# The products with the 16 meta keys in softmax attention: one stacked product of 96 rows for both heads

## The chip, the cores and the metric

One of the eight cores of a Trainium2 chip runs the whole program. The metric is the device time of one execution in microseconds, the median of several runs. The kernel before takes 2984.65 us (2983.28 to 2986.08 in 3 runs).

## The reference, cut to what matters

The program computes two blocks of a language model on 512 tokens, with 16 meta tokens in front, in float32. The first block has two layers (DEPTH = 2). In each, four branches of width 256 are computed from one projection: A, a windowed attention with a sink and a bias; B, an attention with rotary positions; C, a differential attention (two softmaxes, the second subtracted with the factor lam); D, a gated linear attention. In A, B and C every query sees the 16 meta keys beside its own keys. For A this reads

```python
s_b = jnp.einsum('bnqhgd,bnkhd->bhgnqk', qb, kb).astype(jnp.float32) * scale + head_bias(rel_b)
s_m = jnp.einsum('bnqhgd,bmhd->bhgnqm', qb, km).astype(jnp.float32) * scale + head_bias(rel_m)
p = jax.nn.softmax(jnp.concatenate([s_b, s_m, s_sink], axis=-1), axis=-1).astype(v.dtype)
p_b = p[..., :3 * BLOCK]
p_m = p[..., 3 * BLOCK:3 * BLOCK + N_META]
o = jnp.einsum('bhgnqk,bnkhd->bnqhgd', p_b, vb) + jnp.einsum('bhgnqm,bmhd->bnqhgd', p_m, vm)
```

and B and C are softmax attention over all 528 keys. Each has four query heads and two key and value heads of 64. The second block has a windowed attention of its own (kind W) without meta keys.

## The kernel before

The tokens are cut into tiles (TILES): four of 128 and, last, one of the 16 meta tokens; layer 1 leaves the meta tile out as a query tile. The list `att` has one entry for each step of the softmax attention: a query tile and a pair of heads, one for each of the two key heads (j = 0, 1). A layer runs all steps of C, then of A, then of B: 30 steps in layer 0 and 24 in layer 1. Kind C has four cells a step (two softmaxes for each head), A and B have two. A cell is one row of scores for a query, its meta part first (16 columns) and then the other keys.

The engines walk the same list, each in its own order, tied by semaphores. Every engine executes its instructions in the order written.

TensorE (`attention`, L1776 on) makes at step n the scores of n (`scores`, L1633; for B and C the scores against the meta keys by a product of its own at L1644, for both heads at once), then the values products of n - 2 (`values`, L1687), then turns the probabilities of n - 1 (`turn_probs`, L1657): a transpose of the 16 meta columns of each head (L1681) into bank 5 of the accumulators, and one transpose for each 128 other keys (L1684) into bank 4. Then it fills up with products of other branches (`fill_piece`, L1728, 24 products of fp32r type at L1742 to L1750), and at last come the transposes of the second head. Around B, `turn_heads` (L1714) turns the rotated queries and keys of one tile per step through bank 7.

In `values`, 128 keys at a time of both heads are multiplied with the values (128 rows, 64 columns of weights, so that the two heads lie beside one another in the array), and then, for the last group, the 16 meta keys of each head (16 rows): `v` is the values' part in the work buffer, and `x` is PT for the 128-row groups and PTM for the meta group (L1709, L1710). All of it is plain fp32, each product in two passes, hence two records in the trace. At odd steps the reciprocals of the sums are spread first (L1696). Elsewhere in the kernel exact products are made of three fp32r ones: the operand is split into a high part (rounded to fp32r) and a low part (the difference).

ScalarE (`attention`, L2587 on) makes the exps (L2503), copies the turned probabilities into PT (L2517, first and second head) and right after the first head's copy the turned meta probabilities of both heads into PTM, a part of the buffer `cross` (L2520), then copies the finished group (L2526), the fills and the turned heads (`copy_heads`, L2529), and rounds weights (L2243).

VectorE (`attention`, L3377 on) makes at step n the ratios of the sums (L3321, L3324) and, in C, the difference of the two softmaxes (L3335) of step n - 1, the meta scores (L3301, L3306) and their minimum (`meta_scores`, L3293, one reduce at L3309 for all cells), one minimum for each cell with the scores written beside it (`minima`, L3285), the scaling of a finished group (L3359), then rotary work (L3252 to L3267), gates and the low halves of weights (L2935). GpSimd has the rotary products (L1213 to L1220).

## Time and profile before

| | |
|---|---|
| median of 3 runs | 2984.65 us |
| lowest, highest | 2983.28, 2986.08 us |
| span of the profiled execution | 2989.1 us |
| softmax attention of layer 0 | about 99 to 292 us |
| softmax attention of layer 1 | about 1153 to 1322 us |

How to read it: the page gives busy time of every engine, the chain of work that ended last, and groups of instructions by line. PE is TensorE's products, PEld its weight loads, DVE VectorE, ACT ScalarE, POOL GpSimd, SP SyncE. Products are pipelined, so two records in a row overlap: the distance of their starts, not their duration, is what one costs. The rows on which the prediction rests are in a section of their own.

### The profile page before, as it was taken

Reading aid. Unit: us, or ns where it says so; the run is one execution under the profiler, and the core shown is the slowest. Engines: PE = TensorE matmul, PEld = TensorE weight load, DVE = VectorE, ACT = ScalarE, POOL = GpSimd, SP = SyncE. Lnnn points to the kernel's source line nnn. Section 1 sums busy time; section 2 is a strip of 40 time slices with the busy share of each in tenths; the row PEclk is TensorE's granted clock in tenths of the full one; section 3 lists DMA queues with packets and bytes.
Section 4 is the critical chain, followed back from the end, with each engine's and each line's share of the span. In section 5 each row is a group of like instructions: output and inputs, shape, how many; then the busy total and the mean of one; then the engine's idle time right before and its main releaser. Section 6 shows DMA issues by size and latency. Waiting matters only on the chain.

```text
span 2989.1 us, 56782 instructions
## 1 busy us (share of the span) xinstructions
PE 2927.0 (98%) x23600; PEld 2632.0 (88%) x23600; DVE 1900.7 (64%) x3660; ACT 1134.5 (38%) x2022; POOL 377.3 (13%) x610
## 2 busy tenths in 40 slices
PE   9999999999999999999999999999999999999998
PEld 8777999999999998789999899987888885799997
DVE  5564677557777746646865766677536655685565
ACT  4655233232212235552323434434222222554353
POOL 0242433000000020323320000002000000000000
PEclk9999999999999999999999999999999999999999
DMA  6725766244555574347533444438723431134442
GB/s 207 212 49 143 182 149 165 73 141 158 196 189 169 196 213 127 72 131 190 148 114 121 151 143 152 162 115 214 185 93 135 141 121 43 57 115 157 148 174 85
DMA packets 119511, 428.65 MB, mean 143 GB/s; under 512 B 14248, under 2 KB 16680, under 8 KB 114264
## 3 DMA queue, kind: packets, MB, share of 16 engines
q1 hardware_dynamic: 67032, 261.50, 25.6%
q0 software_dynamic: 52224, 163.51, 20.7%
q8 instruction: 189, 3.10, 0.4%
q14 instruction: 66, 0.54, 0.1%
HBM read 414.34 MB, written 109.01 MB: 175 GB/s over the span
## 4 chain that ended last, share of the span: by engine, by line
PE 88%; DVE 4%; ACT 4%; issue 2%; DMA 1%; POOL 1%; SPq 0%; DVEq 0%; ACTq 0%; POOLq 0%
PE acc L1382 13%; PE acc L1383 13%; PE acc L1384 13%; PE acc L1835 5%; PE acc L1836 5%; PE acc L1837 5%; PE acc L2101 4%; PE acc L2102 4%; PE acc L2103 4%; ACT temps L2503 2%; PE acc L1710 2%; PE acc L1651 1%; PE acc L1417 1%; PE acc L2119 1%; PE acc L1901 1%
## 5 line engine op out<-in xcount | busy, mean ns | idle before, releaser
L2243 ACT ACTIVATE toep_r<-ring 128x1024 fp32r<-128x1024 f32 (+2 forms) x216 | 251.4, 1165 | 327.6 <-PE acc L1384 327.6
L1383 PE MATMUL acc<-normed_r,toep_r 128*128 128x264 f32 (+2 forms) x1120 | 357.0, 319 | 0.0
L2935 DVE TENSOR_TENSOR ring_r<-ring,toep_r 128x1024 fp32r<-128x1024 f32 (+2 forms) x212 | 289.4, 1366 | 96.1 <-ACT toep_r L2243 95.5
L1384 PE MATMUL acc<-work_r,ring_r 128*128 128x264 f32 (+2 forms) x984 | 323.6, 329 | 0.0
L1835 PE MATMUL acc<-residual_r,toep_r 128*128 128x264 f32 (+1 forms) x1024 | 301.0, 294 | 1.6 <-DVE mixed L3359 1.6
L1836 PE MATMUL acc<-normed_r,toep_r 128*128 128x264 f32 (+1 forms) x1024 | 292.2, 285 | 0.0
L1837 PE MATMUL acc<-residual_r,ring_r 128*128 128x264 f32 (+1 forms) x1024 | 291.3, 284 | 0.0
L1382 PE MATMUL acc<-work_r,toep_r 128*128 128x264 f32 (+2 forms) x828 | 268.4, 324 | 0.6 <-DVE ring_r L2945 0.6
L1383 PE MATMUL acc<-work_r,toep_r 128*128 128x264 f32 (+2 forms) x720 | 231.5, 321 | 0.0
L1383 PEld LDWEIGHTS acc<-normed_r,toep_r 128*128 128x128 f32 x1120 | 210.6, 188 | 14.5
L1835 PEld LDWEIGHTS acc<-residual_r,toep_r 128*128 128x128 f32 x1024 | 195.5, 191 | 8.0 <-DVE mixed L3359 1.9
L1382 PE MATMUL acc<-mixed_r,toep_r 128*128 128x264 f32 x704 | 202.5, 288 | 0.0
L1384 PEld LDWEIGHTS acc<-work_r,ring_r 128*128 128x128 f32 x984 | 185.1, 188 | 17.3
L1384 PE MATMUL acc<-mixed_r,ring_r 128*128 128x264 f32 x704 | 199.5, 283 | 0.0
L1836 PEld LDWEIGHTS acc<-normed_r,toep_r 128*128 128x128 f32 x1024 | 195.7, 191 | 1.5
L2649 ACT ACTIVATE toep<-acc 128x264 f32<-128x264 f32 (+1 forms) x128 | 49.6, 388 | 386.8 <-PE acc L1837 386.8
L1837 PEld LDWEIGHTS acc<-residual_r,ring_r 128*128 128x128 f32 x1024 | 196.1, 192 | 0.0
L1382 PEld LDWEIGHTS acc<-work_r,toep_r 128*128 128x128 f32 x828 | 155.7, 188 | 13.7 <-issue 1.2
L1382 PE MATMUL acc<-temps_r,toep_r 128*128 128x512 f32 (+1 forms) x416 | 157.0, 377 | 0.7 <-DVE ring_r L2935 0.7
L1384 PE MATMUL acc<-temps_r,ring_r 128*128 128x512 f32 (+1 forms) x416 | 155.4, 374 | 0.0
L2503 ACT ACTIVATE temps<-temps,small 128x528 f32<-128x528 f32 (+6 forms) x176 | 113.3, 644 | 91.0 <-DVE small L3285 90.8
L1383 PEld LDWEIGHTS acc<-work_r,toep_r 128*128 128x128 f32 x720 | 135.4, 188 | 10.5
(614 smaller groups left out, 8117.3 us busy)
## 6 DMA issues: line engine op xcount, KB each, us to landing
ring<-in_w_pair SPq DMA_DIRECT2D x120, 512.0 KB, 3.8
sums_store<-in_w_pair POOLq DMA_DIRECT2D x80, 512.0 KB, 8.8
ring<-in_w_gb SPq DMA_DIRECT2D x64, 640.0 KB, 4.5
ring<-in_w_down SPq DMA_DIRECT2D x32, 704.0 KB, 4.2
lower_store<-in_w_pair POOLq DMA_DIRECT2D x20, 1024.0 KB, 10.4
sums_store<-sums_store POOLq DMA_DIRECT2D x40, 512.0 KB, 5.1
extra<-in_w_ada POOLq DMA_DIRECT2D x18, 1024.0 KB, 6.0
toep<-in_w_ada POOLq DMA_DIRECT2D x18, 1024.0 KB, 6.3
```

Source lines behind the costliest of these rows:

```text
L1382: mm(out, wh, xh[:, a:z], start=i == 0, stop=False)
L1383: mm(out, wh, xl[:, a:z], start=False, stop=False)
L1384: last = mm(out, wl, xh[:, a:z], start=False, stop=end)
L1835: mm(out, wh, xh[:, a:z], start=m == 0, stop=False)
L1836: mm(out, wh, xl[:, a:z], start=False, stop=False)
L1837: last = mm(out, wl, xh[:, a:z], start=False, stop=m == len(xs) - 1)
L2101: mm(out, wh, xh, start=begins and k == 0, stop=False, skip_group_check=True)
L2102: mm(out, wh, xl, start=False, stop=False, skip_group_check=True)
L2103: last = mm(out, wl, xh, start=False, stop=k == 3, skip_group_check=True)
L2243: A(high(ld), slot(ld), ACT.Copy).then_inc(S["w_high"], 1)
L2503: A(x, x, ACT.Exp, bias=negm[0:rows, i:i + 1], scale=-1.0, accum_out=sums[0:rows, i:i + 1]).then_inc(S["att_exp"], 1)
L2935: V.tensor_tensor(low(ld), slot(ld), high(ld), ALU.subtract).then_inc(S["w_low"], 1)
```

## The change

The two heads' meta probabilities are laid beside one another, so that one transpose turns both. For this the first head (j = 0) keeps its meta columns behind the other keys and the second head (j = 1) in front of them; the end of one row of the scores buffer and the start of the next are then 32 neighbouring columns. In C the order of the cells of the first head is reversed for the same reason.

The turned 32 rows (16 for each head) are put into a buffer of 96 rows of fp32r type, PTMR: rows 0 to 31 and 64 to 95 the rounded probabilities (two copies on ScalarE), rows 32 to 63 the rest, the exact value less the rounded one (`low_probs`, one subtract on VectorE). The values are stacked to match, VTMR, once for each kind and layer: rows 0 to 63 the rounded values, rows 64 to 95 their low halves, with the two heads in the left and right 64 columns. Then one fp32r product of 96 rows and 128 columns of weights adds high x high, low x high and high x low for both heads, where there were two fp32 products of 16 rows. The stack of values is made on TensorE by a product with a selection matrix PICK (`stack_values`): for C and A at the first step of C, for B in `turn_heads` of the meta tile. ScalarE rounds it and copies an exact part (`high_values`, two copies for each kind), VectorE makes the low half (`low_values`). The exact part VEXACT is one buffer for all kinds.

The constants get 192 more columns for PICK. The head statistics of C and of D share semaphores now; this changes no order.

```diff
+        metas = sb("metas", 5 * P)
...
-        PTM = cross[0:META, :].rearrange("p (i c) -> p i c", i=2)
+        metas_r = rounded("metas")
+        PTMR = metas_r[0:6 * META, 0:P]
+        VTMR = {kind: metas_r[0:6 * META, P + P * i:2 * P + P * i] for i, kind in enumerate("CAB")}
+        VEXACT = metas[4 * META:6 * META, 4 * P:5 * P]
+        PICK = part(con, CONSTS, "pick", META).rearrange("p (j c) -> p j c", j=2)
...
+                        w = META + hi - lo
+                        key0, meta0, from_ = (META, 0, 0) if j else (0, hi - lo, L - w)
+                        heads.append([((META if j else L - w) + P * b, values_of(s, v, j)) for b, s in enumerate(tiles)] +
                                      [(0, values_of(NT - 1, v, j))])
...
+                                if x0 == 0 and (j or hi - lo == 384):
+                                    c["sums"] = [(0, w, AB[0:rows, h, 0:w])]
+                                else:
+                                    c["sums"] = [(meta0, META, far if x0 == 0 else AM[0:rows, h, int(a == 0), :]),
+                                                 (key0, hi - lo, AB[0:rows, h, near + x0:near + x0 + hi - lo])]
...
                 if c["marked"]:
                     if n and att[n - 1]["metas0"]:
-                        pe.wait_ge(S["att_ptm"], att[n - 1]["metas0"])
+                        pe.wait_ge(S["att_ptl"], att[n - 1]["metas0"])
...
-                    for i in range(2):
-                        turn(PS[0:META, 5, P * i:P * i + rows], of(i)[:, 0:META], ident[0:rows, 0:rows])
+                    joined = (c["kept"] + (c["kind"] == "C") + 1) * L
+                    turn(PS[0:2 * META, 5, 0:rows], T[0:rows, joined - META:joined + META], ident[0:rows, 0:rows])
...
+                if c["metas"] and n == layers[c["l"]]["C"][0]:
+                    pe.wait_ge(S["metas_high"], 3 * c["l"] + 2)
                 pe.wait_ge(S["att_pt"], 2 * n + 2)
-                if c["metas"]:
-                    pe.wait_ge(S["att_ptm"], c["metas0"] + 1)
-                k = len(c["heads"][0])
+                k = len(c["heads"][0]) - c["metas"]
                 for b in range(k):
                     for j in range(2):
-                        v = c["heads"][j][b][1]
-                        x = PT[j][:, b, 0:rows] if v.shape[0] == P else PTM[:, j, 0:rows]
...
+                if c["metas"]:
+                    if n == layers[c["l"]][c["kind"]][0]:
+                        pe.wait_ge(S["metas_low"], 3 * c["l"] + "CAB".index(c["kind"]) + 1)
+                    pe.wait_ge(S["att_ptl"], c["metas0"] + 1)
+                    last = mm(PS[:, 6, P * i:P * i + rows], VTMR[c["kind"]], PTMR[:, 0:rows], start=False, stop=True,
+                              skip_group_check=True)
                 last.then_inc(S["att_pv"], 1)
+
+            def stack_values(kind, out):
+
+                for j in range(2):
+                    last = mm(out[:, 64 * j:64 * j + 64], PICK[:, j, :], values_of(NT - 1, meta_values[kind], j), start=True, stop=True,
+                              skip_group_check=True)
+                return last
...
+                    if n == first and not gated:
+                        if l:
+                            pe.wait_ge(S["y_ready"], layers[0]["groups"])
+                        for i, kind in enumerate("CA"):
+                            last = stack_values(kind, PS[0:6 * META, 6, P * i:P * i + P])
+                        last.then_inc(S["metas_made"], 1)
...
                 if j == 0 and c["metas"]:
-                    A(PTM[:, :, 0:rows], PS[0:META, 5, 0:256].rearrange("p (i c) -> p i c", i=2)[:, :, 0:rows], ACT.Copy
-                      ).then_inc(S["att_ptm"], 1)
+                    A(PTMR[0:2 * META, 0:rows], PS[0:2 * META, 5, 0:rows], ACT.Copy)
+                    A(PTMR[4 * META:6 * META, 0:rows], PS[0:2 * META, 5, 0:rows], ACT.Copy).then_inc(S["att_ptm"], 1)
+
+            def high_values(kind, x):
+
+                A(VTMR[kind], x, ACT.Copy)
+                A(VEXACT, x[4 * META:6 * META, :], ACT.Copy).then_inc(S["metas_high"], 1)
...
+                    act.wait_ge(S["metas_low"], 3 * l + 2)
+                    high_values("B", PS[0:6 * META, 7, 3 * P:4 * P])
                 A(BK[:, a:z], PS[:, 7, 256:256 + z - a], ACT.Copy).then_inc(S["b_heads_ready"], 1)
...
+                    if ly and n == first:
+                        act.wait_ge(S["metas_made"], ly["l"] + 1)
+                        for i, kind in enumerate("CA"):
+                            if 3 * ly["l"] + i:
+                                act.wait_ge(S["metas_low"], 3 * ly["l"] + i)
+                            high_values(kind, PS[0:6 * META, 6, P * i:P * i + P])
...
-                link(V.tensor_reduce(metamin[0:rows, 0:k], out, AX, ALU.min))
+                if c["kind"] == "C":
+                    V.tensor_reduce(metamin[0:rows, 0:2], out[0], AX, ALU.min)
+                    link(V.tensor_reduce(metamin[0:rows, 2:4], out[1], AX, ALU.min))
+                else:
+                    link(V.tensor_reduce(metamin[0:rows, 0:2], pair, AX, ALU.min))
...
+            def low_probs(c):
+
+                rows = c["rows"]
+                dve.wait_ge(S["att_ptm"], c["metas0"] + 1)
+                V.tensor_tensor(PTMR[2 * META:4 * META, 0:rows], PS[0:2 * META, 5, 0:rows], PTMR[0:2 * META, 0:rows],
+                                ALU.subtract).then_inc(S["att_ptl"], 1)
+
+            def low_values(l, kind):
+
+                dve.wait_ge(S["metas_high"], 3 * l + "CAB".index(kind) + 1)
+                V.tensor_tensor(VTMR[kind][4 * META:6 * META, :], VEXACT, VTMR[kind][4 * META:6 * META, :], ALU.subtract
+                                ).then_inc(S["metas_low"], 1)
...
                         copy_second(att[n - 1])
+                    if ly and n == first:
+                        low_values(ly["l"], "C")
+                        low_values(ly["l"], "A")
+                    if ly and first <= n - 1 < end:
+                        low_probs(att[n - 1])
+                    if ly and n == ly["turn_step"] + NT:
+                        low_values(ly["l"], "B")
                     if first <= n - 2 and att[n - 2]["i"]:
```

## Rows read from the trace of the kernel before

**Rows 1.** The page: busy time of each engine.
```profile
PE 2927.0 (98%) x23600; PEld 2632.0 (88%) x23600; DVE 1900.7 (64%) x3660; ACT 1134.5 (38%) x2022; POOL 377.3 (13%) x610
```
**Rows 2.** Chain of waits, branch C, layer 0: start us, us, what.
```profile
144.81 2.27 ACT temps L2503 x6
...
150.98 0.75 DVE temps L3285
151.77 2.27 ACT temps L2503 x6
```
**Rows 3.** Chain of waits, values products of A and B, both layers.
```profile
174.35 1.18 PE acc L1710 x20
...
255.43 1.39 PE acc L1710 x20
...
1309.83 1.24 PE acc L1710 x20
```
**Rows 4.** Timeline, TensorE, a B step of layer 0: start us, us, instruction.
```profile
262.53 1.04 PE L1710 MATMUL acc<-mixed,work 128*64 128x128 f32 x16
...
263.50 0.43 PE L1710 MATMUL acc<-cross,work 16*64 16x128 f32 x4
...
263.87 0.39 PE L1681 MATMUL acc<-con,temps 128*16 128x128 f32 x2
264.09 0.60 PE L1684 MATMUL acc<-con,temps 128*128 128x128 f32 x4
```
**Rows 5.** Timeline, TensorE, windowed attention of the second block.
```profile
2552.52 0.61 PE L1710 MATMUL acc<-mixed,work 128*64 128x128 f32 x8
2553.06 0.66 PE L1684 MATMUL acc<-con,temps 128*128 128x128 f32 x4
```
**Rows 6.** Timeline and chain: fp32r products of 64 and 264 moving columns.
```profile
337.06 0.53 PE L1880 MATMUL acc<-con_r,work_r 16*128 16x64 f32 x4
337.51 0.34 PE L1934 MATMUL acc<-toep,work 64*64 64x64 f32 x4
...
244.10 0.12 PE acc L1748
```
**Rows 7.** Timeline of a C step, then groups: small copies and reduces.
```profile
154.43 0.36 ACT L2520 ACTIVATE cross<-acc 16x256 f32<-16x256 f32 x1
154.69 0.36 ACT L2526 ACTIVATE mixed<-acc 128x256 f32<-128x256 f32 x1
...
L2541 ACT ACTIVATE work<-acc 128x128 f32<-128x128 f32 x4 | 1.1, 274 | 0.0
...
L3309 DVE TENSOR_REDUCE small<-temps 128x4 f32<-128x64 f32 x16 | 3.5, 220 | 0.6
...
L3309 DVE TENSOR_REDUCE small<-temps 128x2 f32<-128x32 f32 x16 | 3.0, 186 | 0.5
```
**Rows 8.** Chain of waits, the exps of the first and third C step, both layers.
```profile
102.45 3.00 ACT temps L2503 x8
...
115.63 2.27 ACT temps L2503 x6
...
1156.14 3.00 ACT temps L2503 x8
...
1169.57 2.27 ACT temps L2503 x6
```
**Rows 9.** Timeline, TensorE, second C step of layer 0: [idle before <-releaser].
```profile
107.73 0.38 PE L1681 MATMUL acc<-con,temps 128*16 128x128 f32 x2 [1.74 <-DVE temps L3301]
```
**Rows 10.** Stretches: busy us of each engine, granted clock, DMA share, GB/s.
```profile
176.00:180.00 4.00, 4.00 (x20) 3.69 (x19) 3.60 (x16) 1.72 (x7) 0.72 (x2) 0.50 0.00 0
...
1160.00:1164.00 4.00, 2.58 (x13) 2.53 (x14) 3.93 (x12) 1.64 (x5) 0.00 (x0) 0.61 0.10 39
...
1202.00:1263.00 61.00, 58.76 (x564) 47.58 (x562) 38.11 (x115) 35.89 (x108) 26.95 (x28) 1.00 0.29 62
```
**Rows 11.** Timeline, TensorE, the first B scores of layer 1.
```profile
1263.02 0.41 PE L1644 MATMUL acc<-con,work 128*128 128x32 f32 x2 [0.65 <-ACT work L2541]
```

More of the change, by code:

```diff
@@ L121, in constants @@
     c["Z0"], c["Z1"] = r > t, r < t
+    c["pick"] = np.zeros((P, 12 * META))
+    for i in range(3):
+        for j in range(2):
+            at = (6 * j + 2 * i + j) * META
+            c["pick"][:META, at:at + META] = np.eye(META)
     consts = np.concatenate([np.asarray(c[n], np.float32) for n in CONSTS], 1)
@@ new lines, in layer_attention @@
+                        for comp in ((0, 1) if j else (1, 0)) if kind == "C" else (0,):
+                            wide = 32 if kind == "C" else 64
+                            r = slice(64 * j + 32 * comp, 64 * j + 32 * comp + wide)
+                            c = dict(q=q[i][r, a:z], head=j, sums=[], scores=[(0, k[r, lo:hi])], width=w, from_=from_,
+                                     at=from_ if kind == "A" else key0)
+                            if kind == "A":
+                                c["scores"] = [(meta0, k[r, 0:META]), (key0, k[r, lo:hi])]
+                                far = AB[0:rows, h, 0:META] if j else AB[0:rows, h, 384:]
+                                near = META if j else 0
+                                if x0 == 0 and (j or hi - lo == 384):
[3 more added lines that the diff above has]
+                                                 (key0, hi - lo, AB[0:rows, h, near + x0:near + x0 + hi - lo])]
@@ L1019, in build @@
                     r, h = slice(64 * j, 64 * j + 64), i + 4 * j
-                    cells.append(dict(q=Q2[i][r, c0:c0 + P], head=j, scores=[(0, K2[r, lo:c0 + P])], width=w,
+                    cells.append(dict(q=Q2[i][r, c0:c0 + P], head=j, scores=[(0, K2[r, lo:c0 + P])], width=w, from_=0, at=0,
                                       sums=[(0, w, ALIBI[:, h, 2 * P - w:2 * P])]))
@@ L1722, in turn_heads @@
                                 ident[0:z - a, 0:z - a])
+                if t == NT - 1:
+                    last = stack_values("B", PS[0:6 * META, 7, 3 * P:4 * P])
                 last.then_inc(S["rope_turned"], 1)
@@ L1821, in head_spread @@
                                           ident[0:z - a, c0 - a:c1 - a], start=True, stop=True, skip_group_check=True)
-                last.then_inc(S[kind + "_spread"], 1)
+                last.then_inc(S["heads_spread"], 1)
             def gate_piece(ly, q):
@@ L2501, in exps @@
                 act.wait_ge(S["att_min"], c["cell0"] + g + 1)
-                x, i = SB[0:rows, c["kept"] + g, 0:w], 4 * (n % 4) + g
+                first = c["cells"][g]["from_"]
+                x, i = SB[0:rows, c["kept"] + g, first:first + w], 4 * (n % 4) + g
                 A(x, x, ACT.Exp, bias=negm[0:rows, i:i + 1], scale=-1.0, accum_out=sums[0:rows, i:i + 1]
@@ L3295, in meta_scores @@
                 n, rows, k = c["n"], c["rows"], len(c["cells"])
-                out = SB[0:rows, c["kept"]:c["kept"] + k, 0:META]
+                out = [SB[0:rows, c["kept"]:c["kept"] + 2, L - META:L], SB[0:rows, c["kept"] + 2:c["kept"] + 4, 0:META]]
+                joined = (c["kept"] + 1) * L
+                pair = T[0:rows, joined - META:joined + META].rearrange("p (h m) -> p h m", h=2)
                 if c["kind"] == "C":
@@ L3333, in difference @@
                 for j in range(2):
-                    p0, p1 = (SB[0:rows, c["kept"] + 2 * j + comp, :] for comp in range(2))
+                    p0, p1 = (SB[0:rows, c["kept"] + x, :] for x in (1 + j, 3 * j))
                     V.scalar_tensor_tensor(out=p0, in0=p1, scalar=cfac[0:rows, 2 * (n % 4) + j:2 * (n % 4) + j + 1],
```

68 lines of the change are left out of this document (33 added, 35 removed).

## The prediction

> **What bounds the kernel now.** I read the page first. TensorE is busy for 98% of the span [rows 1], so a microsecond taken off another engine is worth nothing unless TensorE waits for it. The change touches only the two softmax attention stages (about 99 to 292 us in layer 0 and 1153 to 1322 us in layer 1), 362 us of 2989. There I read the chain of waits, then the timeline of single steps. A step is one query tile with one pair of heads.
>
> The chain has two regimes. In branch C it does not run over TensorE: the last exp of one step releases VectorE (ratios, difference, meta scores, first minimum), that releases three exps, then come the copy of the turned probabilities, the copy of the turned meta probabilities and the fourth exp, which closes the ring [rows 2]. The three exps start at 144.81 and again at 151.77, 6.96 us a step. From the end of C on, the chain runs over TensorE: in B of layer 0 the values products start at 255.43 and, in the next step, after 262.5, and between them lie only TensorE pieces, fill products included; the last such piece of layer 1 is at 1309.83 [rows 3]. So an instruction saved on TensorE counts in A and B, and one added to ScalarE or VectorE counts in C.
>
> **TensorE, removed.** Today the values products of a full step are 16 records of 128 rows, then 4 records of 16 rows (two heads, two passes each), then two meta transposes. The starts are 262.53, 263.50, 263.87 and 264.09 [rows 4]: the 16 rows' part takes 0.37 us and each transpose 0.11. 16 records take 0.97, some 0.06 each. The change replaces the 0.37 by one fp32r product of 96 rows, 128 columns of weights and 128 moving columns, and drops one transpose. A values group that goes straight to 128-wide transposes is seen in the later windowed attention: 8 records, 0.54 us from the first start to the transpose [rows 5]; 16 would take 0.54 + 8 x 0.06 = 1.02. The old sequence takes 0.97 + 0.37 + 0.22 = 1.56 up to the big transposes, the new one 1.02 + x + 0.11. It saves 0.43 - x.
>
> No row shows x. From below: four fp32r records with 128 columns of weights and only 64 moving columns take 0.45, so 0.11 each, and a 264-column one takes 0.12 [rows 6]. From above: a pair of concurrent fp32 products of this width takes 0.24 (a quarter of 0.97) [rows 4]. The 64-column row can mean a floor of 0.11 that 128 columns do not leave, or a rate four times lower for narrow operands (64 x 4 / 2.4 GHz = 0.107), which makes 128 columns 0.21. Nothing in the rows decides; I take 0.21, the careful end, and keep 0.11 for the range. The saving is 0.22 per step (0.32 with the floor).
>
> A rule of the Trainium skill bears on this. "TensorE: Matmul & The Clock Gate", LDWEIGHTS, gives a weight load as its columns over 1.2 GHz, whatever the rows: 128 columns are 0.107, which agrees with the 64-column row [rows 6]. By it x is 0.11 and the change comes out on the first rival below.
>
> Which steps count: full ones whose values group lies in the chain on TensorE. There are 15 such pieces in layer 0 from 174.35 on (two more lie where the chain leaves TensorE for the rotary work on VectorE and GpSimd) and 19 in layer 1, the last but two at 1309.83 [rows 3]. Two of the 34, at the end of B, start only after a wait for a copy of ScalarE, so I count 32. The steps of the 16-row tile save next to nothing. Gain: 32 x 0.22 = **7.0 us**.
>
> **Added on the ring of C.** The meta copy costs the ring 0.26 today (154.43 to 154.69) [rows 7]. It becomes two copies of 32 x 128. A copy of 128 x 128 takes 0.27 against 0.36, and the next one starts some 0.09 before the end, so 0.18 each: +0.10. The one meta reduce becomes two; one of half the size takes 0.19 against 0.22, with its tail covered: +0.08. That is 0.18 a step on 16 of the 18 C steps (the first of each layer is costed below, its last is TensorE's): **+2.9 us**. The new VectorE subtract for the low halves comes after the minima, when VectorE waits for the fourth exp anyway, so I cost it at nothing there; if the cover is gone it is 0.2 a step, 3.6 us.
>
> **Added at the start of each layer.** In the first step ScalarE now makes four copies after its fill copy, and VectorE two subtracts, as a chain by turns, because both kinds go through one exact buffer: two copies (0.45), a subtract (0.2), two copies, a subtract, with some 0.1 for each of four handovers. That is 1.7 us. Queued behind it on VectorE are the ratios and the difference, which now start as soon as the fourth exp is done, at 105.45 [rows 8]. The ring is late by that: **+3.4 us** for both layers. TensorE idles 1.74 us there now [rows 9] and would idle 3.4. In layer 1 the clock fell to 0.61 right after this idle piece [rows 10]. The first two rings took 13.43 us there (1156.14 to 1169.57) and 13.18 in layer 0 (102.45 to 115.63), where it did not fall [rows 8]: 0.25 for a fall, as TensorE has room in C. **+0.4** for both.
>
> **Added around B.** turn_heads for the meta tile gets two small fp32 products of 16 rows (4 records; nearest are the 4 records at 0.37 [rows 4]), on TensorE's path in both layers. ScalarE gets two copies ahead of the one that frees the bank. In layer 0 nearly two steps lie between it and the first user that waits. In layer 1 TensorE idles 0.65 us for exactly this copy before the first B scores [rows 11], so they count, 0.4. Sum 2 x 0.4 + 0.4 = **+1.2 us**. The low-half subtracts also go ahead of the rotary work on VectorE where that is late in layer 0; there are two such steps, which I counted neither as a gain nor, at 0.2 each, as a loss. The extra split minimum in two A steps a layer, the 98 KB of constants (loaded while TensorE is packed) and the renamed semaphores I cost at nothing: TensorE's own work covers them; bare, the minima would be 1 us.
>
> **Added waits.** TensorE's meta scores and meta transposes now wait for VectorE's subtract instead of ScalarE's copy. In C that subtract would end some 0.8 after the meta copy's start, at 155.2 on the scale of [rows 7], before the fourth exp is through, and nobody needs the scores before that; in B it is older by a whole step. Behind the waiting subtract on VectorE stand weight splits and the rotary work, which already waited for ScalarE's group copy on every second step.
>
> **The sum.** -7.0 + 2.9 + 3.4 + 0.4 + 1.2 = **+0.9 us** on the profiled execution's 2989.1 us span, which lies 4.45 us above the median of 2984.65. The median becomes 2985.5. A measurement of this kernel can tell about 0.2%, 6 us, from no change.
>
> **Rivals.**
> 1. The fp32r product is cheap (x = 0.11). The gain is 32 x 0.32 = 10.2, the sum -2.3, the time 2982. For it is the equal price of 64 and 264 columns, against it only that 64 x 4 cycles fits as well.
> 2. Faster outright: x is 0.11, and the start chain and the C copies hide (ScalarE's gap before the exps grows without moving the ring), and the clock does not fall at the change from C to A in layer 0. It is at 0.50 in 176 to 180 us [rows 10]; a fill is 24 products of 0.12, 2.9 us, and twice that at half speed. That is -10.2 + 2 + 1.2 - 2.9, about 2975.
> 3. Slower: the emptier TensorE. In C a step gets longer and TensorE's work in it shorter by about 0.4. If the clock falls in TensorE's own regime in layer 1 too (full speed there now [rows 10]), each fall costs a fill at half speed, 2.9 us; two or three of these give +6 to +8, 2992. It decides where a wait of TensorE near the end of C reaches the 1.74 us of [rows 9], after which the clock fell in one layer and stood in the other.
> 4. The new subtract is not covered in C and A (it waits for a copy that waits for TensorE): +3.6 and some steps of A, 2990.
> 5. The change does not do what it says, since TensorE is not the bound where I see it so: only the costs remain, +7.9, 2993.
>
> **How the numbers follow.** Forecast (within 3 us of 2985.5) 0.38, rival 1 0.27, rival 2 0.09, rival 3 0.12, rival 4 0.09, rival 5 0.05. Both of the likeliest lie within 0.2%. The range takes in x at both ends, the start chain at half and at double price, and rivals 1, 3 and 4: 2978 to 2993. Faster by over 0.2% 0.12 (rival 2 and the lower tail of 1), slower 0.19 (rivals 3 and 5, a quarter of 4), the same 0.69.
>
> **What would show it.** One record of 96 rows between the values group and a single transpose, at a distance of 0.11 or 0.21. Each B step shorter by 0.2 to 0.3. The C ring at 7.1 to 7.2 for 6.96. The first ring of each layer 1.7 us longer, with ScalarE and VectorE by turns. The clock's row at 104 to 112 and 1204 to 1220. I am wrong if the ring of C does not lengthen, if the A and B steps gain 0.4 or nothing, or if the difference comes from outside the attention stages.

## The result, and the profile after

| | before | after |
|---|---|---|
| median, first comparison (5 runs each) | 2985.58 us | 2997.66 us, ratio 1.0036 (95%: 1.0025 to 1.0046) |
| median, second comparison (11 and 7 runs) | 2987.39 us | 2996.22 us, ratio 1.0027 (1.0016 to 1.0039) |
| span of the profiled execution | 2989.1 us | 2995.0 us |

The change makes the kernel 9 to 12 us slower. The forecast was 2985.5, range 2978 to 2993: wrong. The spans differ by less, 5.9 us, because the profiled execution of the kernel before is one of its longer ones: by e8 below (span 2990.1, time 2991.91) its time would be about 2991. The page of the changed kernel says little, as TensorE is still busy nearly all the time, 192 of its records fewer, and ScalarE and VectorE are each busy for some 16 us more [rows 1]:

```profile
PE 2918.6 (97%) x23408; PEld 2629.0 (88%) x23408; DVE 1917.3 (64%) x3746; ACT 1150.2 (38%) x2088; POOL 376.3 (13%) x610
```

The stages say more. The first exp of each C step stands in the chain of waits. Here are the first and the third to eighth of layer 0 in the changed kernel (start us, us, what):

```profile
102.20 2.99 ACT temps L2548 x8
...
118.28 2.27 ACT temps L2548 x6
...
125.60 2.27 ACT temps L2548 x6
...
134.01 2.27 ACT temps L2548 x6
...
141.92 2.27 ACT temps L2548 x6
...
149.50 2.27 ACT temps L2548 x6
...
156.82 2.27 ACT temps L2548 x6
```

From 118.28 to 125.60 and from 149.50 to 156.82 it is 7.32 us, where [rows 2] had 6.96. The rings between them differ in length, as they hold other work besides (8.41 from 125.60 to 134.01), but each is longer than its own counterpart by 0.35 to 0.37. The exception, in this layer and at one place in layer 1, is a ring with a weight split, here 134.01 to 141.92: 7.91, where that ring was 6.96 too. The first two rings, 102.20 to 118.28, take 16.08 us against 13.18 [rows 8]. I call the distance from one step's first exp to the next one's its ring.

For a sum over both layers I compare, step by step, the start of the score products on TensorE (L1651 before, L1676 after) in two traces. From the second C step to the last B step of each layer the changed kernel loses, in us (C is counted up to the second step of A, as the last steps of C overlap the first of A):

| | C, layer 0 | A and B, layer 0 | C, layer 1 | A and B, layer 1 | sum |
|---|---|---|---|---|---|
| changed kernel, first trace | +6.5 | -1.5 | +4.7 | -2.4 | +7.3 |
| changed kernel, second trace (e11) | +6.1 | -1.7 | +5.4 | -0.8 | +9.1 |
| kernel before, second trace (e8) | +0.2 | +0.5 | -0.3 | 0.0 | +0.5 |

The two attention stages carry 7 to 9 of the 9 to 12 us. Outside them the same code differs from trace to trace: from the last B step of layer 0 to the second C step of layer 1 the kernel before takes 2.0 us more in its second trace than in its first, with nothing changed.

### The profile page after: what moved, and what is told of

The parts are those of the page before. It is cut to its first block, busy times and chain, and to the rows that moved or that the text cites. A ratio compares the mean times of both kernels' runs of the same rounds, so it can differ in the third digit from the quotient of the medians.

```text
span 2995.0 us, 56530 instructions
## 1 busy us (share of the span) xinstructions
PE 2918.6 (97%) x23408; PEld 2629.0 (88%) x23408; DVE 1917.3 (64%) x3746; ACT 1150.2 (38%) x2088; POOL 376.3 (13%) x610
## 4 chain that ended last, share of the span: by engine, by line
PE 86%; DVE 5%; ACT 4%; issue 2%; DMA 1%; POOL 1%; SPq 0%; DVEq 0%; ACTq 0%; POOLq 0%
PE acc L1407 13%; PE acc L1408 13%; PE acc L1409 13%; PE acc L1879 5%; PE acc L1880 5%; PE acc L1881 5%; PE acc L2145 4%; PE acc L2146 4%; PE acc L2147 4%; ACT temps L2548 2%; PE acc L1442 1%; PE acc L1676 1%; PE acc L2163 1%; PE acc L1733 1%; PE acc L1924 1%
```

## The experiments

All times of a group stand beside runs of the kernel before on the same chip (2988.35 us for e1 to e4, 2988.58 for e5 to e8, 2987.39 for e9 to e12). "Rings" are the two rings of layer 0 that [rows 2] stands for (the third and the seventh, 6.96 before); "sum" is the last column of the table above, from one profiled execution each. e8 and e12 are one execution each and have no interval. In the text, theory 1, theory of the forecast and rival are those of the expectation in front of each run.

| | median us | ratio to before (95%) | rings | sum |
|---|---|---|---|---|
| e1 start unchained | 2992.90 | 1.0017 (1.0008 to 1.0026) | 7.32 | +3.4 |
| e2 one copy in C | 2990.97 | 1.0012 (1.0003 to 1.0020) | 6.91 | +4.0 |
| e3 meta scores last in B | 2998.91 | 1.0033 (1.0020 to 1.0045) | 7.32 | +8.6 by the exps |
| e4 old way in C | 2990.07 | 1.0011 (1.0003 to 1.0020) | 7.02 | +3.1 |
| e5 new way, repaired | 2983.98 | 0.9980 (0.9970 to 0.9990) | 6.85 | -3.9 |
| e6 old C, new A and B | 2987.29 | 0.9991 (0.9982 to 0.9999) | 6.96 | -1.9 |
| e7 e6, copy on VectorE | 2981.47 | 0.9976 (0.9967 to 0.9985) | 6.96 | -5.4 |
| e8 kernel before again | 2991.91 | one execution | 6.96 | +0.5 |
| e9 e5, split first | 2978.94 | 0.9967 (0.9955 to 0.9980) | 6.85 | -8.7 |
| e10 e9, late meta scores | 2977.31 | 0.9965 (0.9952 to 0.9977) | 6.85 | -6.8 by the exps |
| e11 changed kernel again | 2996.22 | 1.0027 (1.0016 to 1.0039) | 7.32 | +9.1 |
| e12 second copy elsewhere | 2996.56 | one execution | 7.07 | +6.3 |

e3 and e10 put the meta scores behind the score products, so there the start of the score products comes earlier in a step and no longer marks the same point; in these two the sum goes by the first exp of the last B step. In all other runs the two ways agree within 0.02 us. A sum and a median of the same run need not agree to the microsecond: e5's profiled execution is the fastest of its 12 (2976.80), e7's the slowest of its 11 (2987.30).

**e1: the start of a layer.**

```diff
-        VEXACT = metas[4 * META:6 * META, 4 * P:5 * P]
+        VEXACT = {kind: metas[4 * META:6 * META, P * at:P * at + P] for kind, at in (("C", 4), ("A", 3), ("B", 4))}
...
-                            if 3 * ly["l"] + i:
-                                act.wait_ge(S["metas_low"], 3 * ly["l"] + i)
+                            if ly["l"]:
+                                act.wait_ge(S["metas_low"], 3)
...
-                    if ly and n == first:
+                    if ly and n == first + 1:
                         low_values(ly["l"], "C")
```

> Edit: the changed kernel, but its start of a layer is unchained: ScalarE copies the stacked values of C and of A one after the other into places of their own (the exact copy of A's lies where B's stacked values come later), without waiting for VectorE in between, and VectorE takes both remainders one step later, behind the minima of the second C step. Nothing is left out. Theory 1 (the start chain 105.36 to 107.14 stands in the first ring of both layers, and the granted clock falls behind TensorE's wait): the first ring of layer 0, first exp to first exp, goes from 8.20 us back to 6.9..7.3, the second, 7.88, to 7.3, the clock stays at 1.00 in it, layer 1 gives about 2 of its peak of +4.7; in all -3.5 to -6, so 2992 to 2994. Rival 2 (the loss is carried by TensorE's clock or by the stacked product, the start only takes slack): first ring 7.9 or more and 2996 to 2999. Rival 3 (VectorE's two remainders in the second step take the place of the chain): first ring short, second ring over 7.9, total gain under 1.5.

In the changed kernel the timeline of ScalarE, then of VectorE, shows the chain by turns after the fourth exp (start us, us, engine, line, instruction, [idle before <-releaser]):

```profile
105.36 0.26 ACT L2570 ACTIVATE metas_r<-acc 96x128 fp32r<-96x128 f32 x1
105.62 0.27 ACT L2571 ACTIVATE metas<-acc 32x128 f32<-32x128 f32 x1
106.24 0.27 ACT L2570 ACTIVATE metas_r<-acc 96x128 fp32r<-96x128 f32 x1 [0.35 <-DVE metas_r L3421]
106.53 0.27 ACT L2571 ACTIVATE metas<-acc 32x128 f32<-32x128 f32 x1
...
105.92 0.28 DVE L3421 TENSOR_TENSOR metas_r<-metas,metas_r 32x128 fp32r<-32x128 f32 x1 [1.75 <-ACT metas L2571]
106.83 0.28 DVE L3421 TENSOR_TENSOR metas_r<-metas,metas_r 32x128 fp32r<-32x128 f32 x1 [0.62 <-ACT metas L2571]
107.14 0.18 DVE L3386 RECIPROCAL small<-small 128x4 f32<-128x4 f32 x1
```

The ratios wait for the second subtract and begin at 107.14. In e1 they begin at once behind the fourth exp, and ScalarE's four copies lie beside them:

```profile
102.65 3.00 ACT temps L2548 x8
...
105.67 0.19 DVE small L3386
...
108.93 2.27 ACT temps L2548 x6
```

That is e1's chain of waits: the first ring is 6.28 us, against 8.20 in the changed kernel (102.20 to 110.40) and 6.22 before. In both layers the chain cost 1.92 us, more than theory 1 gave back (its ring was 6.9 to 7.3). The second ring, 7.88 in the first trace of the changed kernel, is 7.46 in e1. The stretches of this time (behind the stretch and its length come TensorE's busy time and, third from the end, its granted clock) are, first in the kernel before, then in the changed kernel, then in e1:

```profile
104.00:108.00 4.00, 1.77 (x13) 0.89 (x14) 2.83 (x10) 1.71 (x6) 1.57 (x2) 1.00 0.78 121
108.00:112.00 4.00, 3.82 (x34) 3.65 (x32) 2.65 (x8) 3.33 (x9) 0.00 (x0) 1.00 1.07 126
```

```profile
104.00:108.00 4.00, 1.74 (x13) 0.69 (x11) 1.53 (x7) 2.42 (x9) 1.44 (x2) 0.91 0.92 156
108.00:112.00 4.00, 2.60 (x13) 2.63 (x14) 3.93 (x13) 1.60 (x5) 0.00 (x0) 0.50 1.05 128
```

```profile
104.00:108.00 4.00, 2.25 (x18) 1.24 (x17) 2.85 (x10) 2.87 (x11) 0.89 (x1) 1.00 0.96 188
108.00:112.00 4.00, 3.52 (x30) 3.35 (x30) 3.35 (x12) 3.04 (x9) 0.00 (x0) 1.00 0.92 112
```

In the changed kernel TensorE waits 3.66 us here ([rows 9]: 1.74 before), as its own timeline shows:

```profile
109.40 0.37 PE L1706 MATMUL acc<-con,temps 128*32 128x128 f32 x1 [3.66 <-DVE temps L3362]
```

In and behind this wait the granted clock falls to 0.50, the lower of its two levels, 1.2 GHz. In e1 the wait is 1.75 us and the clock stands at 1.00. The other runs do not make this a rule. e5 has e1's start, the same wait of 1.75, and TensorE is busy for 2.26 us in 104 to 108, for e1's 2.25. Yet its clock falls:

```profile
108.00:112.00 4.00, 3.99 (x21) 4.00 (x22) 3.38 (x11) 3.03 (x9) 0.00 (x0) 0.57 0.95 120
```

So it does in e6 and e7 (waits of 1.73 and 1.74, clock 0.59 and 0.57), while it stands before, in e8, e9 and e10 with the same wait. With the wait of 3.66 it falls in layer 0 of every one of the traces of the changed kernel, e2, e3, e4 and e12, but by different amounts: in e11 it is 0.80 in 108 to 112, and the second ring is 7.45, no longer than e1's 7.46. So the longer wait and the fall go together in layer 0, the price here was 0.4 us in one trace and nothing in another, and what decides whether the clock falls stays open.

Theory 1 holds for the chain, and the time of 2992.90 lies in its span.

**e2: one copy in C.**

```diff
-                    A(PTMR[4 * META:6 * META, 0:rows], PS[0:2 * META, 5, 0:rows], ACT.Copy).then_inc(S["att_ptm"], 1)
+                    if c["kind"] != "C" or c["n"] == layers[0]["C"][0]:
+                        ins_ = A(PTMR[4 * META:6 * META, 0:rows], PS[0:2 * META, 5, 0:rows], ACT.Copy)
+                    ins_.then_inc(S["att_ptm"], 1)
```

> Edit: the changed kernel, but in kind C ScalarE copies the 32 turned meta rows once a step and not twice (the first C step alone still writes rows 64 to 96), so in C the product high probabilities x low values works on old rows: that part of C's result is left out. Theory 1 (C is bound by the chain over ScalarE, and each of its small copies costs its whole 0.26 to 0.29 us): C rings 7.32 -> 7.04 in both layers, times 16 less the first, about -4.3 us: 2993.4. Theory of the forecast (0.10 a copy): rings 7.22, -1.6: 2996. Rival (rings lengthened by the reduces and the wait for the subtract, copies hidden): rings stay at 7.3, 2997 to 2998.

The rings are 6.91 us, 0.41 shorter: more than theory 1 said (0.28), and four times the forecast's price. (The sum falls by 3.3 us only, as this trace has two falls of the clock in A and B, 0.70 in 204 to 208 us and 0.57 in 1264 to 1268, with steps 1.2 and 1.5 us longer than in the changed kernel.) ScalarE's timeline shows where it goes. In the changed kernel from the first meta copy to the fourth exp:

```profile
152.15 0.25 ACT L2565 ACTIVATE metas_r<-acc 32x128 fp32r<-32x128 f32 x1
152.41 0.27 ACT L2566 ACTIVATE metas_r<-acc 32x128 fp32r<-32x128 f32 x1
152.70 0.73 ACT L2548 ACTIVATE temps<-temps,small 128x528 f32<-128x528 f32 x1
```

and in e2:

```profile
150.75 0.25 ACT L2565 ACTIVATE metas_r<-acc 32x128 fp32r<-32x128 f32 x1
150.91 0.72 ACT L2548 ACTIVATE temps<-temps,small 128x528 f32<-128x528 f32 x1
```

By the starts the one copy costs 0.16, its last 0.09 under the next instruction; the pair costs 0.26 + 0.29 = 0.55. The kernel before paid 0.26 [rows 7].

**e12: the second copy to the same partitions.** Why does a second copy cost 0.39 when the first costs 0.16?

```diff
-                    A(PTMR[4 * META:6 * META, 0:rows], PS[0:2 * META, 5, 0:rows], ACT.Copy).then_inc(S["att_ptm"], 1)
+                    other = c["kind"] == "C" and c["n"] > layers[0]["C"][0]
+                    to = metas_r[0:2 * META, 4 * P:4 * P + rows] if other else PTMR[4 * META:6 * META, 0:rows]
+                    A(to, PS[0:2 * META, 5, 0:rows], ACT.Copy).then_inc(S["att_ptm"], 1)
```

> Edit: the changed kernel, but in C ScalarE's second copy of the 32 turned rows goes to 32 rows of the same partitions (0 to 31) beside them, and not to partitions 64 to 95; as in e2 the product high probabilities x low values of C is thereby made of old rows. Theory 1 (any second small copy in a row costs 0.39 us, whatever its partitions): C rings stay at 7.32. Rival (the move to other partitions is what keeps the copies from overlapping): the pair takes 0.32 in place of 0.55 us and the rings are 7.07 to 7.1.

The rival wins, to the hundredth: the rings are 7.07, and the pair takes 0.32 (from the first copy's start to the exp's; 0.55 in the changed kernel):

```profile
152.10 0.25 ACT L2565 ACTIVATE metas_r<-acc 32x128 fp32r<-32x128 f32 x1
152.26 0.25 ACT L2568 ACTIVATE metas_r<-acc 32x128 fp32r<-32x128 f32 x1
152.42 0.72 ACT L2548 ACTIVATE temps<-temps,small 128x528 f32<-128x528 f32 x1
```

So the dear thing was not a copy but that its output begins at partition 64 where its neighbours' outputs begin at 0: neither it nor the exp behind it starts under its predecessor's tail. That is 0.23 of the 0.39. The Trainium skill ("VectorE: DVE Perf Modes", Two Vector instructions with no wait between them) states that a VectorE instruction whose output starts in another group of 32 partitions than the last one's waits for its predecessors' end. Here ScalarE does the like: in the changed kernel the first copy runs from 152.15 to 152.40, and the second starts at 152.41.

**e3: the meta scores last in B.**

```diff
-                if c["marked"]:
+                def with_metas():
...
+                if c["marked"] and c["kind"] == "C":
+                    with_metas()
...
                 if c["kind"] != "C":
+                    if c["marked"]:
+                        last = with_metas()
```

> Edit: the changed kernel, but in kind B the product for the meta scores is issued behind the two cells' score products and not ahead of them, so that its wait for VectorE's subtract holds up none of them. Nothing is left out. Theory 1 (in B's steps without a fill TensorE waits 1.0 to 1.35 us for the subtract in front of this product, 0.55 to 0.60 before the change): these waits shrink to under 0.7 in some four steps of each layer, -1 to -3 us: 2995 to 2996.5. Rival (the same wait is met one product later, since minima and meta minima need both): no step shortens, 2997 to 2998, and the idle time stands ahead of the product as before.

The rows behind the theory are TensorE's waits in front of this product in B's last steps. First the kernel before, then the changed one:

```profile
272.38 0.38 PE L1644 MATMUL acc<-con,work 128*128 128x32 f32 x2 [0.55 <-issue]
277.38 0.22 PE L1644 MATMUL acc<-con,work 128*16 128x32 f32 x2 [0.55 <-issue]
282.09 0.22 PE L1644 MATMUL acc<-con,work 128*16 128x32 f32 x2 [0.60 <-issue]
```

```profile
276.60 0.38 PE L1669 MATMUL acc<-con,work 128*128 128x32 f32 x2 [1.25 <-issue]
281.78 0.22 PE L1669 MATMUL acc<-con,work 128*16 128x32 f32 x2 [1.04 <-issue]
286.79 0.22 PE L1669 MATMUL acc<-con,work 128*16 128x32 f32 x2 [1.34 <-issue]
```

The wait is real: by the score starts these steps cost the changed kernel 0.39, 0.18 and 0.31 in layer 0 and 0.38 in layer 1. In e3, measured by the exps, three of them are 0.65, 0.19 and 0.98 shorter in layer 0 and one is 0.93 shorter in layer 1, but four earlier full steps of B in each layer, where TensorE is the bound, are 0.18 to 0.20 longer; why is not known. The sum is +8.6 against +7.3; a fall of the clock (0.72 in 1268 to 1272 us) makes one B step of layer 1 1.8 us longer than in the changed kernel and hides what is left of the gain. The time does not move beyond its interval. Theory 1 was right in the place; the gain of 1 to 3 us that it forecast is not seen. e10 below takes only the late steps.

**e4: the old way in C.** Two transposes, one copy, two fp32 products, no subtract; the start of a layer keeps its new work.

```diff
+                    if c["kind"] == "C":
+                        for i, col in enumerate((L - META, 0)):
+                            turn(PS[0:META, 5, P * i:P * i + rows], of(i)[:, col:col + META], ident[0:rows, 0:rows])
```

> Edit: the changed kernel, but in kind C each step goes the way of before: two transposes of 16 columns, one copy to 16 rows x 256, two fp32 products of 16 rows, no subtract; A and B keep the new way, and the start of the layer its new work. Nothing is left out. Theory 1 (two regimes: in C the change costs, in A and B it saves): C rings 7.32 -> 7.0, the rings with a weight split 7.91 -> 7.0, about -6.5 us, so 2991; A and B lose nothing. Rival (C has slack, the loss sits in A, B and the starts): rings stay, 2997. Rival (the two C products in fp32 cost TensorE 0.43 a step that shows): 2999 or more.

Rings 7.02, the ring with the split 7.02 in place of 7.91: theory 1. Against the 6.96 of [rows 2] the two reduces are left, 0.06. The start chain is still there (first ring 8.20): 4.0 of the 5.3 us that C still loses. A and B repeat the changed kernel's steps to 0.02 us, but for the first ones of each layer and one more in layer 1.

**e6 and e7: old C, new A and B.** e6 adds to e4 the unchained start without a stack for C, and one reduce in place of two. e7 gives ScalarE's second copy in A and B to VectorE, behind the subtract.

```diff
-                    A(PTMR[4 * META:6 * META, 0:rows], PS[0:2 * META, 5, 0:rows], ACT.Copy).then_inc(S["att_ptm"], 1)
...
                                 ALU.subtract).then_inc(S["att_ptl"], 1)
+                V.tensor_copy(PTMR[4 * META:6 * META, 0:rows], PTMR[0:2 * META, 0:rows]).then_inc(S["att_ptm"], 1)
```

> Edit: the changed kernel, with the old way in every C step (as e4), no stacked values for C at the start of a layer, those of A unchained as in e1, and one reduce in place of two in C. A and B as in the changed kernel. Nothing is left out. Theory 1 (C's part of the change is pure cost, A's and B's gives 4 to 5 us over both layers): C as in the kernel before (rings 6.96, first 6.2), A and B as in the changed kernel, so 3 to 5 us below before (0.9983 to 0.999). Rival (what A and B seem to save is given back behind the attention): within 0.05% of before.

> Edit: e6, and in A and B ScalarE's second meta copy goes to VectorE, behind the subtract (as in e5). Nothing is left out. Theory 1 (B's steps without a fill wait for the chain copy, copy, subtract): the last four or five B steps of each layer 0.25 shorter, two A steps of each layer that VectorE sets 0.2 longer: 1 to 2 us below e6. Rival (VectorE sets more steps than ScalarE does): 0 to 1.5 us above e6.

e6 has the kernel before's C rings to 0.01 us, but for the second ones (7.44 for 6.96 in layer 0, with the clock at 0.79 in 104 to 112 us), and gains 2.5 us in A and B, a little less than theory 1. e7's sum is 3.5 us lower. 1.3 of it is one step at the turn from C to A: the clock fell to 0.50 in both, and from 180 to 184 us it is 0.63 in e6 and 0.99 in e7. The other 2.1 are the copy: B's last steps in layer 0 change by +0.11, -0.11 and +0.12 against before in place of +0.39, +0.18 and +0.31; one more step of B in each layer now gains its 0.30; and a rotary step of A that lost 0.63 in the changed kernel and in e6 loses 0.02. VectorE's copy, 0.22 us, shows in no step. The medians of e6 and e7 are 5.8 us apart; the traces account for these 3.5, and the rest is not assigned.

**e5: the new way everywhere, repaired.** e1, one reduce, and the copy of e7 in C too.

```diff
-                    V.tensor_reduce(metamin[0:rows, 0:2], out[0], AX, ALU.min)
-                    link(V.tensor_reduce(metamin[0:rows, 2:4], out[1], AX, ALU.min))
+                    four = bass.AP(base.tensor, base.offset, [list(base.ap[0]), [L + META, 2], [L, 2], [1, META]])
+                    link(V.tensor_reduce(metamin[0:rows, 0:4].rearrange("p (a b) -> p a b", a=2), four, AX, ALU.min))
```

> Edit: the changed kernel with all of its new way in C, A and B, and four repairs: the unchained start of e1; one reduce over all four meta parts of a C step in place of two; ScalarE copies the 32 turned rows once, VectorE takes the low part first and releases the meta bank with it, and copies the high rows 0 to 32 to rows 64 to 96 behind that. Nothing is left out. Theory 1 (the cost of the change is ScalarE's second copy in the ring, the second reduce and the start chain, all of it incidental): C rings 6.9 with VectorE's copy under cover, first ring 6.3, B's last steps 0.26 shorter each, A's steps bound by VectorE 0.2 longer each; in all 5 to 8 us below the kernel before (ratio 0.9975 to 0.9985). Rival (VectorE is as much on the C ring as ScalarE, so the moved copy costs there what it saved): C rings 7.2, and a time within 2 us of before (0.9995 to 1.0007).

The rings are 6.85, below the 6.96 of before: one copy of 32 x 128 costs the ring 0.16 where the old 16 x 256 cost 0.26. The rival falls. But the ring with a weight split is still 7.83 in each layer.

**e9: the weight ahead of the metas.**

```diff
+                    early = splits_at.get(n - 1, ()) if ly and mixed and first < n <= end else ()
+                    for ld in early:
+                        low_weights(ld)
                     if ly and first <= n - 1 < end:
                         low_probs(att[n - 1])
```

> Edit: e5, and in a C step that also splits a weight, VectorE makes the low part of the weight ahead of the low part of the turned metas. Nothing is left out. Theory 1 (in these rings VectorE first waits 0.95 to 1.23 us for ScalarE's meta copy and only then does 1.2 us of weight, so that the ratios come late): the rings of 7.83 us, one in layer 0 and one in layer 1, fall to 6.9 to 7.0, -1.8 us against e5; nothing else changes. Rival (the weight's ring is long because of the weight itself): 7.8 stays, though the kernel before has its weights in rings of 6.96.

In the changed kernel VectorE's timeline in such a ring is

```profile
137.22 0.28 DVE L3415 TENSOR_TENSOR metas_r<-acc,metas_r 32x128 fp32r<-32x128 f32 x1 [1.23 <-ACT metas_r L2566]
137.53 1.22 DVE L2994 TENSOR_TENSOR ring_r<-ring,work_r 128x1024 fp32r<-128x1024 f32 x1
138.67 0.17 DVE L3386 RECIPROCAL small<-small 128x4 f32<-128x4 f32 x1
```

and in e9

```profile
132.10 1.22 DVE L2993 TENSOR_TENSOR ring_r<-ring,work_r 128x1024 fp32r<-128x1024 f32 x1
133.34 0.28 DVE L3415 TENSOR_TENSOR metas_r<-acc,metas_r 32x128 fp32r<-32x128 f32 x1
```

The weight fills the time in which the other order waited. The rings of 7.83 fall to 6.91 and 6.90. What theory 1 had not seen: the ring before falls too, from 8.15 to 7.24 in both layers, which is below the 8.04 of before. The two effects are 0.92 each in each layer, 3.7 us in all; C as a whole is 4.2 us shorter (e5 had +1.0 and +0.1 there, e9 -1.4 and -1.8), the rest being the second ring of layer 0, where e5 had the fall of the clock (7.34 for 6.99), and the turn to A. e9 is 8.5 us faster than the kernel before.

**e10: the meta scores last, in B's late steps only.**

```diff
+                late = c["kind"] == "B" and n - layers[c["l"]]["B"][0] >= 6
```

> Edit: e9, and the product for the meta scores is issued behind the score products as in e3, but only in the steps of B without a fill (from its seventh). Nothing is left out. Theory 1 (e3 gained in these steps, 4.95 -> 4.30, 5.25 -> 5.06, 4.66 -> 3.68 in layer 0, and lost 0.18 to 0.20 in each of the earlier ones): the early steps as in e5, the late ones 1 to 1.5 us shorter in layer 0 and 0.5 to 0.8 in layer 1; 1.5 to 2.3 us below e9. Rival (e5 has already taken that wait, by releasing the bank 0.26 earlier): under 0.5 us.

By the exps, layer 0's three late steps are 1.1 us shorter than in e9 and the one before them 0.2 longer. In layer 1 a fall of the clock (0.50 in 1256 to 1260 us) lies over them. The medians of e9 and e10 are 1.6 us apart, and each ratio lies inside the other's interval: not settled, and small.

**e8 and e11: both kernels again.**

> The kernel before, unchanged, for a second trace. Theory 1: the fall of the granted clock at 504 to 512 us that the first trace of it has, and the trace of the changed kernel has not, is chance; with it or without it, every ring and step of both layers' attention repeats within 0.05 us. Without the fall the span is 2986 to 2987. Rival (the change removed the fall): the fall stands at 504 to 512 again, and the span is 2988 to 2990.

> The changed kernel, unchanged, beside the kernel before on this chip, for a second trace and a narrower interval. Theory 1 (both layers' attention carries +7 to +8 us, the rest is chance outside it): ratio 1.0024 to 1.0036, every ring within 0.05 us of the first trace but the second of a layer, which depends on the clock. Rival (a further 3 to 5 us of the change sit outside the attention): 1.0036 to 1.0046 and a stretch outside it that is longer in both traces of the changed kernel than in both of before.

The ring lengths of C and the step lengths of A and B repeat to 0.03 us in e8 and in e11, but for the second rings and the steps that lie on or right behind a fall of the clock. A fall at 504 to 512 us in the first trace of before,

```profile
504.00:508.00 4.00, 2.88 (x34) 2.64 (x35) 3.92 (x20) 0.69 (x3) 3.50 (x11) 0.69 0.32 114
508.00:512.00 4.00, 4.00 (x20) 4.00 (x20) 1.09 (x8) 0.00 (x0) 1.93 (x3) 0.50 0.94 279
```

is there again in e8, as the rival said, with a span of 2990.1, and neither trace of the changed kernel has it. But e1 and e3, which have the changed kernel's C, do have it (0.50 and 0.57 at 512 to 516), and e5 has not. Whether the change touches it stays open; by an estimate from these rows (0.31 and 0.50 of 4 us each) it would be up to 3 us in the change's favour, and it explains none of the loss. In e11 the clock fell twice in layer 1, behind TensorE's waits at the start of C and of B (3.66 and 1.23 us, the same as in the first trace, where it stayed at 1.00 at the start of B), and the steps there took 0.7 and 1.6 us longer than in the first trace. Less the 0.4 by which layer 0's second ring is shorter, that is the difference of the two sums. The ratio of e11 fits theory 1, and its sum of 9.1 accounts for its 8.8 us: no part of this loss has to be looked for outside the attention stages. Of the 12 us of the first comparison the first trace's sum accounts for 7.3; the rest is not assigned.

## Why the prediction was wrong, point by point

The terms of the sum beside the first trace. In C they come from the rings; in A and B from the score starts, the first line from all steps that became shorter, the second from all that became longer:

| term | forecast | measured |
|---|---|---|
| product and transpose in A, B | -7.0 | -6.5 |
| around B, in A (measured: every longer step) | +1.2 | +2.6 |
| C, 14 rings (12 by 0.30 to 0.37, and 0.36 in each second ring) | +2.9 | +5.0 |
| C, two rings with a weight split, 0.95 each | as any ring | +1.9 |
| start chain, 1.98 a layer | +3.4 | +4.0 |
| clock behind it | +0.4 | +0.4 |
| sum | +0.9 | +7.4 |

**The product was cheaper than taken, in fewer steps.** In a B step of the changed kernel TensorE's records are

```profile
266.66 1.04 PE L1733 MATMUL acc<-mixed,work 128*64 128x128 f32 x16
267.63 0.33 PE L1739 MATMUL acc<-metas_r 96*128 96x128 f32 x1
267.80 0.27 PE L1706 MATMUL acc<-con,temps 128*32 128x128 f32 x1
267.91 0.60 PE L1709 MATMUL acc<-con,temps 128*128 128x128 f32 x4
```

beside those of [rows 4]: from the values' start to the big transpose 1.25 us for 1.56. The saving is 0.31, seen in 17 steps within 0.02. Of my two ends for x the lower was right: 0.43 - 0.31 = 0.12. A rate four times lower for narrow operands, the reading behind 0.21, would have left a saving of 0.22. The choice of 0.21 was the careful one and not the one nearest to a row of four equal records [rows 6]. The Trainium skill's rule ("TensorE: Matmul & The Clock Gate", LDWEIGHTS) gives 0.107 for the load of 128 columns, which agrees. But only 17 of my 32 steps gained in full. The others gained less or nothing: in A around the rotary work, in B in one step a layer that e7 frees by moving the copy, and in the late steps. A gain that rival 1 had sized at -10.2 with this x became -6.5; that it lies so near to the -7.0 of the forecast is luck, as a saving taken too small met a count of steps taken too large. The count of "pieces in the chain on TensorE" was not a count of steps in which TensorE was the only bound.

**The step that failed first: the meta copy in C, +0.10.** The two copies cost 0.55 where the one of before cost 0.26, so +0.29. I took the price from wide copies, 128 x 128 with a tail of 0.09 under the next instruction. The price per column was right (0.16 in e12), but the change of output partitions between neighbours adds 0.23, and no row of before had such a neighbour. This is a bound that I should have put above the row and did not: over 14 C rings the 0.19 more than forecast is 2.7 us. The reduces were +0.06, forecast +0.08.

**The second: the subtract "costed at nothing".** It is covered where VectorE has nothing else to do. I had named weight splits behind it in the queue and stopped there, as they "already waited". In the two rings with a split it cost 0.95 less the 0.36 of any ring: the subtract waits for ScalarE with 1.2 us of work behind it that needed no wait (e9). Rival 4 has this mechanism, at 0.2 a step everywhere; it is 0 in most steps and 0.6 in two, 1.2 us in all.

**The third: "in B it is older by a whole step".** It is not. The product for the meta scores of step n waits until the metas of n - 2 are read, and these were turned only one TensorE step earlier. ScalarE's second copy and VectorE's subtract now lie in that wait: from 0.55 to 1.04..1.34 us. It showed only where no fill covers it: 0.39, 0.18 and 0.31 in layer 0 and 0.38 in layer 1, 1.3 of the 2.6 us in the table. The other 1.3 are 0.63 in a rotary step of A in layer 0, which e7 frees, 0.63 at the start of B in layer 1, which it does not, and 0.07.

**The start chain** was forecast at 1.7 a layer and is 1.98, with the engines by turns as drawn. The 0.4 for the clock came as sized in the first trace, by +0.56 in layer 0 and -0.11 in layer 1 (where before had a fall of its own); in e11 it is +0.13 and +0.60, so the size is partly luck. Of rival 3, what I called an emptier TensorE, the place was right (behind the wait at the start of C, and in e11 before B), the chance too low. Rival 5 gave the nearest time, 2993, for a wrong reason: A and B did gain.

**Where the range failed.** The copy in C was outside any bound that I had written for it: there was none. The subtract (1.2 us) lies inside rival 4's 3.6, the start chain inside its half to double price, and the wait in B had no price. Nothing in the range added such misses together, and all of them have one sign: every one added a wait or an instruction to the engines that set the pace there, and I had costed those at their bare price in the best order.

## What to carry to other kernels

Where a change takes work from the busiest engine and gives it to the others, ask in each stage who closes the ring there; e6 and e7 show the gain standing alone, in the stages where TensorE is the bound. Put work that needs no wait ahead of work that waits (e9: 3.7 us for the order of two instructions), and give a small copy to the engine that is waiting anyway (e7: 2.1 us). The gain itself is small: where TensorE is the bound a step saves 0.31 us, and e6 is 1.3 us below the kernel before. The changed kernel was 0.3% slower, and the same idea with four repairs, e9, is 0.33% faster than the kernel before.

## What the runs showed of the hardware

- ScalarE: two neighbouring copies of 32 x 128 that begin at the same output partition are 0.16 us apart. With the second output at partition 64, the pair and the next instruction are 0.26 and 0.29 apart (e12 against the changed kernel, rings 7.07 and 7.32).
- TensorE: an fp32r product of 96 rows, 128 columns of weights and 128 moving columns costs 0.12 us in a stream of fp32 work by the prediction's reckoning (the next start comes 0.17 behind its own, of which some 0.05 belong to the records of 128 rows before it), hardly more than one with 64 moving columns [rows 6].
- The granted clock fell to 0.50 behind a wait of 3.66 us of TensorE in the first trace (0.80 in e11). Behind a wait of 1.73 to 1.75 us at the same place it stood in e1, e8, e9, e10 and the kernel before and fell to 0.57 to 0.59 in e5, e6 and e7: the same kernel and the same wait do not always give the same clock. In C such a fall cost nothing (layer 0 of e11), 0.4 us (layer 0 of the first trace) or 0.7 (layer 1 of e11), in B's start 1.6 (e11).
